# Second block's attention: value products issued ahead of the scores two units on

## The chip, the cores and the metric

The kernel is one program on one core of a Trainium2 chip. The metric is the device time of one execution in microseconds (us). The engines are named as in the profile: PE is TensorE (matrix products; PEld is its weight load), DVE is VectorE, ACT is ScalarE, POOL is GpSimd, and SP issues the transfers. Each engine runs its own list of instructions in the order in which the program gives them, and engines wait for each other on semaphores.

## What is computed

Two transformer blocks in a row, each with two layers, all in float32: 256 latent tokens and 256 context tokens, 1024 features. The first block (a gated recurrence, then attention over a compressed key) is not touched. The change is in the attention of the second block, which stands once in each of its two layers. Its reference, cut to what matters:

```python
def latent_attention(q, k, v, kc, vc, sink):          # 8 query heads, 2 key heads, head width 64
    s_lat = einsum(qb, kb) * scale                     # banded: |q - k| <= 128
    s_lat = where(valid, s_lat, NEG_INF)
    s_ctx = einsum(qb, kc) * scale
    p = softmax(concat([s_lat, s_ctx, sink]))          # the sink is one more column
    o = p_lat @ vb + p_ctx @ vc

for l in range(2):
    o = latent_attention(q, k, v, kc, vc, attn_sink[l])
    x = x + g1 * merge_branches(o, pool, fourier, gates, ...)
    if l == 0:
        oc = context_attention(qc, kc, vc, attn_sink[l])   # the context attends to itself
        xc = xc + cg1 * merge_branches(oc, ...)
    x = x + g2 * conv_ffn(...)
```

## The kernel before

The order on every engine is written out by hand; no scheduler moves anything. Activations lie with features on the 128 partitions. Weights come through a ring of buffers that SP fills ahead (`L128` in the rows).

The attention of layer `l` is cut into **units** (`att_units`, L863). A unit is a pair of heads `j` (0 to 3) and a block of 128 query rows `g` (2, 3: latent), or `g == 0`, which holds both blocks of the context. Layer 0 has 12 units, in the order 0, 2, 3 for each `j`, so units 0, 3, 6, 9 are context units; layer 1 has 8, all latent. Each unit goes through these steps:

- scores (PE, `att_scores_tensor`): L892 and L894 for a latent unit, L887 for a context unit, into bank 2+3 or 4+5 of `ps`, by the parity of the unit. They wait for `s_exp` of the unit two before, which had the same banks.
- top (DVE, `att_top_vector`): the row maximum L1672 straight from `ps`, then L1673 and L1674.
- exponentials (ACT, `exps`, L1327 and L1329), into `sc`.
- normalising (DVE, L1682, L1683, L1686), which raises `p_ready`.
- transposes (PE, L984): eight, the four of the first head into bank 6, those of the second into bank 1.
- copies out of these two banks into `PTb`: bank 6 always by ACT (L1342); bank 1 by ACT (L1345) for even units, by DVE (L1693) for odd ones. They raise `pt_kept` and `k_turned`.
- values (PE, `values`, L968): the products with the value rows, from `PTb` into bank 7 or 0. They wait for both copies of their own unit. After the last unit of a pair of heads ACT copies the result out (`heads_out`, L1333).

There is one `PTb`, and one bank for the transposes of each head. So the transposes of unit u+1 wait for the copies of u, and the copies of u+1 for the values of u.

DVE's order in `attend_vector` (L1676) matters here: for unit u it normalises u, then takes the top of u+2, and only then, if u is odd, makes the copy out of bank 1:

```python
                ins.then_inc(p_ready, 1)
                if u + 2 < len(units):
                    att_top_vector(dve, st, l, u + 2)
                if u % 2:
                    dve.wait_ge(pt_full, b["ptf"] + 2 * u + 2)
                    dve.wait_ge(pv_full, b["pv"] + u)
                    V.tensor_copy(PTb[:, 1, :], ps[:, 1, :]).then_inc(k_turned, 1)
```

ACT's order in `attend_scalar` is: exponentials of u+1, copy of bank 6 of u, for even u the copy of bank 1, then `heads_out` where a pair has ended. After its loop over the units PE runs `between()`, the first products of the Fourier branch (L994), ahead of the last unit's values, then the branches (L1007 to L1023) and the merge (L1040, L1052).

Of the kernel before, what the change touches and what calls it, by code (L numbers as in the profile page):

```python
# [42 lines left out]
def raised(n):  # L43


    return n + 1
# [89 lines left out]
def build(nc, w, const, out):  # L136
# [5 lines left out]
    with ctx:  # L142
# [715 lines left out]
        def base(l):  # L858
            return dict(unit=32 + 12 * l, ptf=32 + 24 * l, kt=12 * l, pv=8 + 12 * l, rot=9 + 3 * l, qj=1 + 3 * l, pvk=8 + 4 * l,
                        full=5 * l, act=5 * l, dve=3 + 5 * l, br=12 * l, brd=6 * l, bract=4 * l)  # L860


        def att_units(l):  # L863
            return [(j, g) for j in range(4) for g in ((0, 2, 3) if l == 0 else (2, 3))]
# [4 lines left out]
        def att_out(j):  # L869
            return 7 if j % 2 == 0 else 0  # L870

        def att_scores_tensor(pe, l, u):

            b = base(l)
            j, g = att_units(l)[u]
            bank = att_banks(u)
            if u >= 2:
                pe.wait_ge(s_exp, b["unit"] + u - 1)
            elif u == 1:
                pe.wait_ge(qj_ready, b["qj"] + 3)  # L880
            else:
                pe.wait_ge(qj_ready, b["qj"] + 2)
            head = lambda h2: slice(h2 * 64, h2 * 64 + 64)
            if g == 0:
                for gc in range(2):
                    for h2 in range(2):
                        mm = PE.matmul(ps[:, bank + h2, gc * CTX:gc * CTX + CTX], q_raw[head(h2), j, gc * 128:gc * 128 + 128],  # L887
                                       kb[head(h2), 0:CTX], start=True, stop=True)
            else:
                q0 = CTX * (1 - l) + (g - 2) * 128  # L890
                for h2 in range(2):
                    PE.matmul(ps[:, bank + h2, :], q_raw[head(h2), j, q0:q0 + 128], kb[head(h2), :], start=True, stop=False)  # L892
                for h2 in range(2):
                    mm = PE.matmul(ps[:, bank + h2, (5 - g) * 128:(5 - g) * 128 + 128], ident, amask[:, g - 2, :],  # L894
                                   start=False, stop=True)
            mm.then_inc(s_full, 1)
# [57 lines left out]
        def attend_tensor(pe, l, between):  # L954
            b = base(l)
            units = att_units(l)
            head = lambda h2: slice(h2 * 64, h2 * 64 + 64)

            def values(u):
                j, g = units[u]  # L960
                pe.wait_ge(pt_kept, raised(b["unit"] + u + 1))
                pe.wait_ge(k_turned, b["kt"] + u + 1)
                if j >= 2:
                    pe.wait_ge(pv_kept, raised(b["pvk"] + j - 1))
                nk, nq, q0 = (2, 256, 0) if g == 0 else (4, 128, g * 128)
                for kg in range(nk):
                    for h2 in range(2):
                        mm = PE.matmul(ps[head(h2), att_out(j), q0:q0 + nq], vb[:, kg, head(h2)], PTb[:, h2, kg * nq:kg * nq + nq],  # L968
                                       start=kg == 0, stop=kg == nk - 1)
                mm.then_inc(pv_full, 1)  # L970

            pe.wait_ge(in_dve_kept, b["dve"] + 5 - 2 * l)
            for u, (j, g) in enumerate(units):
                if u + 2 < len(units):
                    att_scores_tensor(pe, l, u + 2)
                if u:
                    values(u - 1)
                pe.wait_ge(p_ready, b["unit"] + u + 1)
                for h2 in range(2):
                    if u:  # L980
                        pe.wait_ge(*((pt_kept, raised(b["unit"] + u)) if h2 == 0 else (k_turned, b["kt"] + u)))
                    for n in range(4):
                        dst = n if g else n % 2 * 2 + n // 2
                        mm = PE.transpose(ps[:, (6, 1)[h2], dst * 128:dst * 128 + 128], sc[:, u % 2, h2, n * 128:n * 128 + 128], ident)  # L984
                    mm.then_inc(pt_full, 1)
            between()
            values(len(units) - 1)
# [117 lines left out]
        def _(pe):  # L1105
# [73 lines left out]
            for l in range(2):  # L1179
                n, c0 = T - CTX * l, CTX * l  # L1180
                norm_tensor(pe, f"mix{l}", lambda k: hT[:, k, :], ones, T)
                in_tensor(pe, l)
                attend_tensor(pe, l, lambda: spectra_tensor(pe, l))
                branches_tensor(pe, l)
                merge_tensor(pe, l)
                out_tensor(pe, l)
                norm_tensor(pe, f"ffn{l}", lambda k: hT[:, k, 0:n], ones, n)
                up_tensor(pe, l)
                pe.wait_ge(conv_ready, FT * (l + 1))
                outer_tensor(pe, f"down{l}", lambda k: hid[:, k, 0:n], n, FT, x_added, XB[f"down{l}"],  # L1190
                             lambda k: pe.wait_ge(hid_ready, raised(FT * l + k + 1)))
# [816 lines left out]
```

## Time and profile before

| | us |
|---|---|
| median of three runs | 2806.47 (2806.2 to 2807.56) |
| the profiled execution | 2807.16 |
| its span in the trace | 2805.4 |
| PE busy in it | 2631.2 (94%) |
| DVE busy | 898.9 (32%) |
| ACT busy | 591.8 (21%) |

The attention of layer 0 lies at about 1484 to 1532 us of the span, that of layer 1 at about 2362 to 2394 us. A line of the timeline gives the start in us, the duration in us, the engine, the line of the kernel, the operation, what it writes and reads, the shape, and how many instructions are merged in it; in brackets stands the idle time of the engine ahead of it and what ended it. The trace counts a float32 matrix product of the program as two records, a transpose as one.

### The profile page before, as it was taken

The page shows a single profiled execution, that of the slowest core. Times are in us where ns is not written, and L with a number is a line of the kernel's source. Part 1 is how long each engine was busy: PE and PEld are TensorE (multiplying, and loading weights), DVE is VectorE, ACT ScalarE, POOL GpSimd, SP SyncE. Part 2 cuts the span into 40 slices and gives each one's busy share as a digit, 9 for nine tenths or more (in the row PEclk, how much of TensorE's full clock was granted, in tenths as well). Part 3 has the DMA queues.
Part 4 walks back from the last instruction along what each step waited for, and adds up shares of the span by engine and source line. Part 5 has one row for each costly group of instructions (what it writes and reads, how often), then busy time and mean ns, then how long its engine had stood idle before and what let it go on. Part 6 is the DMA issues. An engine that isn't in the chain of part 4 may idle for free.

```text
span 2805.4 us, 27549 instructions
## 1 busy us (share of the span) xinstructions
PE 2631.2 (94%) x10670; PEld 1627.7 (58%) x10670; DVE 898.9 (32%) x1457; ACT 591.8 (21%) x1017; POOL 52.9 (2%) x42
## 2 busy tenths in 40 slices
PE   7999999999997878899799999999998989999988
PEld 3556666666665435666566444444443437888877
DVE  2236446446446221353115010132322014113321
ACT  3112222212211111242115000032221013103321
POOL 0000000000000100000000000000000000000000
PEclk9999999999998989999999999999999999999999
DMA  8443343333340313112420222222224222343561
GB/s 296 164 152 120 130 138 129 126 134 142 112 135 1 113 30 105 53 37 75 120 60 1 60 60 90 60 60 75 75 75 118 77 60 61 103 154 102 150 183 57
DMA packets 319687, 280.10 MB, mean 100 GB/s; under 512 B 27601, under 2 KB 298585, under 8 KB 319497
## 3 DMA queue, kind: packets, MB, share of 16 engines
q1 hardware_dynamic: 317866, 274.89, 31.9%
q0 software_dynamic: 1280, 4.20, 0.4%
q8 instruction: 45, 0.74, 0.1%
q10 hardware_dynamic: 479, 0.13, 0.0%
q14 instruction: 17, 0.14, 0.0%
HBM read 278.15 MB, written 1.05 MB: 100 GB/s over the span
## 4 chain that ended last, share of the span: by engine, by line
PE 93%; DVE 4%; ACT 2%; issue 1%; DMA 0%; SPq 0%; ACTq 0%; DVEq 0%
PE ps L1094 16%; PE ps L610 16%; PE ps L735 13%; PE ps L1040 9%; PE ps L619 4%; PE ps L657 4%; PE ps L1074 3%; PE ps L1052 3%; PE ps L398 2%; PE ps L345 2%; PE ps L770 2%; PE ps L942 1%; PE ps L920 1%; PE ps L699 1%; DVE rstd L350 1%; PE ps L847 1%
## 5 line engine op out<-in xcount | busy, mean ns | idle before, releaser
L1094 PE MATMUL ps<-hT,ring_mem 128*128 128x512 f32 (+1 forms) x1408 | 458.2, 489 | 9.8 <-ACT hT L411 9.8
L610 PE MATMUL ps<-hT,ring_mem 128*128 128x512 f32 x1024 | 454.4, 597 | 6.4 <-ACT hT L411 6.4
L735 PE MATMUL ps<-arena,ring_mem 128*128 128x256 f32 (+1 forms) x1160 | 375.1, 487 | 22.6 <-issue 14.8
L1094 PEld LDWEIGHTS ps<-hT,ring_mem 128*128 128x128 f32 x1408 | 269.4, 191 | 198.6 <-issue 178.1
L610 PEld LDWEIGHTS ps<-hT,ring_mem 128*128 128x128 f32 x1024 | 190.8, 191 | 238.8 <-issue 237.0
L735 PEld LDWEIGHTS ps<-arena,ring_mem 128*128 128x128 f32 x1160 | 223.5, 193 | 173.9 <-issue 148.1
L1040 PE MATMUL ps<-hT,ring_mem 128*128 128x512 f32 (+1 forms) x768 | 250.3, 486 | 0.0
L1040 PEld LDWEIGHTS ps<-hT,ring_mem 128*128 128x128 f32 x768 | 146.0, 190 | 101.3 <-issue 91.3
L1760 DVE SCALAR_TENSOR_TENSOR arena<-ps,vecs,arena 128x510 f32<-128x510 f32 (+1 forms) x176 | 100.2, 611 | 314.4 <-ACT arena L1385 308.1
L657 PEld LDWEIGHTS ps<-arena,K_c 128*128 128x128 f32 x896 | 115.6, 193 | 23.6 <-issue 22.9
L1722 DVE TENSOR_TENSOR arena<-ps,arena 128x512 f32<-128x512 f32 (+1 forms) x48 | 26.8, 558 | 291.3 <-PE ps L1052 291.3
L657 PE MATMUL ps<-arena,K_c 128*128 128x128 f32 x896 | 118.1, 286 | 0.0
L1732 DVE SCALAR_TENSOR_TENSOR xT<-ps,mod_b,xT 128x256 f32<-128x256 f32 (+1 forms) x48 | 21.8, 481 | 294.9 <-PE ps L735 225.6
L619 PE MATMUL ps<-ring_mem,hT 128*128 128x256 f32 x512 | 113.0, 379 | 0.0
L619 PEld LDWEIGHTS ps<-ring_mem,hT 128*128 128x128 f32 x512 | 96.2, 190 | 12.4
L332 ACT ACTIVATE hT<-xT 128x512 f32<-128x512 f32 (+1 forms) x56 | 26.4, 554 | 361.9 <-DVE xT L1732 333.4
L1231 ACT ACTIVATE K_c<-arena 128x1024 f32<-128x1024 f32 x56 | 64.0, 1144 | 183.0 <-DVE arena L1491 160.4
L350 DVE RECIPROCAL rstd<-root 128x512 f32<-128x512 f32 (+1 forms) x11 | 30.5, 2771 | 215.7 <-ACT root L337 215.7
L1491 DVE TENSOR_TENSOR arena<-arena 128x1024 f32<-128x1024 f32 x56 | 76.3, 1363 | 64.1 <-PE ps L657 64.0
L1052 PE MATMUL ps<-arena,ring_mem 128*128 128x512 f32 (+1 forms) x256 | 85.2, 486 | 0.0
L1074 PE MATMUL ps<-arena,ring_mem 128*128 128x512 f32 (+1 forms) x256 | 82.9, 486 | 0.0
L1385 ACT ACTIVATE arena<-ps,vecs 128x512 f32<-128x512 f32 (+1 forms) x88 | 46.3, 576 | 173.4 <-PE ps L1094 173.1
(227 smaller groups left out, 2553.3 us busy)
## 6 DMA issues: line engine op xcount, KB each, us to landing
ring_mem<-in_w_mod_dram SPq DMA_DIRECT2D x24, 2048.0 KB, 7.6
ring_mem<-in_w_up_dram SPq DMA_DIRECT2D x88, 512.0 KB, 4.8
ring_mem<-in_hg_w_in_dram SPq DMA_DIRECT2D x40, 1024.0 KB, 5.0
ring_mem<-in_w_in_dram SPq DMA_DIRECT2D x30, 1024.0 KB, 5.4
ring_mem<-in_w_down_dram SPq DMA_DIRECT2D x16, 1408.0 KB, 7.3
ring_mem<-in_ada_w_dram SPq DMA_DIRECT2D x8, 2048.0 KB, 7.7
ring_mem<-in_mla_w_in_dram SPq DMA_DIRECT2D x9, 1024.0 KB, 5.5
ring_mem<-in_ada_w_dram SPq DMA_DIRECT2D x8, 1024.0 KB, 10.4
```

The costliest lines, as they stand in the source:

```text
L350: st.link(V.reciprocal(rstd[:, 0:n], root[:, 0:n]))
L610: mm = PE.matmul(bank, wj[:, k, m * 128:m * 128 + 128], hT[:, k, :], start=k == 0, stop=k == 7)
L619: mm = PE.matmul(bank[:, g * 256:g * 256 + 256], hT[:, k, tok:tok + 128], wj[:, k, :], start=k == 0, stop=k == 7)
L657: mm = PE.matmul(dst, K_c[:, u * 128:u * 128 + 128], comb(Qw, 1 << (term - 1), u), start=True, stop=True)
L735: mm = PE.matmul(ps[:, j, 0:n], wj[:, k, :], src(k), start=k == 0, stop=k == kts - 1)
L1040: mm = PE.matmul(ps[:, j, 0:n], wj[:, k, m * 128:m * 128 + 128], hT[:, k, c0:T], start=k == 0, stop=k == 7)
L1052: mm = PE.matmul(ps[:, 3 + j, 0:n], wj[:, k, m * 128:m * 128 + 128], brT[:, k, c0:T], start=k == k0, stop=k == k1 - 1)
L1074: mm = PE.matmul(ps[:, 2 * j + m, 0:n], wj[:, k, m * 128:m * 128 + 128], yT[:, k, c0:T], start=k == 0, stop=k == 7)
L1094: mm = PE.matmul(ps[:, 2 * j + m, 0:n], wj[:, k, m * 128:m * 128 + 128], hT[:, k, c0:T], start=k == 0, stop=k == 7)
L1231: S.activation(view(K_c, (2 * h, PC // (2 * h)), (h, 2), (1, h)), comb(Kw, h), ACT.Copy).then_inc(kc_ready, 1)
L1491: V.tensor_tensor(comb(Qw, h), comb(Qw, h), view(Tw, (2 * h, n), (PC - h, 2), (0, h), at=h), ALU.mult).then_inc(merged, 1)
L1760: ins = V.scalar_tensor_tensor(dst, src, tap(k, f, part), dst, ALU.mult, ALU.add)
```

## The change

In the loop over the units of `attend_tensor`, the call `values(u - 1)` is put ahead of `att_scores_tensor(pe, l, u + 2)`; before it stood behind it. What each waits for, what each computes, and the order on the other engines stay.

```diff
             for u, (j, g) in enumerate(units):
+                if u:
+                    values(u - 1)
                 if u + 2 < len(units):
                     att_scores_tensor(pe, l, u + 2)
-                if u:
-                    values(u - 1)
                 pe.wait_ge(p_ready, b["unit"] + u + 1)
```

PE's list, before, at the start of layer 0's loop: the transposes of unit 0, scores of 3, values of 0, transposes of 1, scores of 4 (two rows), values of 1, transposes of 2. L984 are transposes, L968 values, L887 or L892 with L894 scores.

```order
269 L984 MATMUL ps<-ident,arena 128x128 x8
270 L887 MATMUL ps<-arena 128x256 x4
271 L968 MATMUL ps<-arena 64x256 x4
272 L984 MATMUL ps<-ident,arena 128x128 x8
273 L892 MATMUL ps<-arena 128x512 x2
274 L894 MATMUL ps<-arena,ident 128x128 x2
275 L968 MATMUL ps<-arena 64x128 x8
276 L984 MATMUL ps<-ident,arena 128x128 x8
```

The same place of the same engine in the changed kernel:

```order
269 L984 MATMUL ps<-ident,arena 128x128 x8
270 L968 MATMUL ps<-arena 64x256 x4
271 L887 MATMUL ps<-arena 128x256 x4
272 L984 MATMUL ps<-ident,arena 128x128 x8
273 L968 MATMUL ps<-arena 64x128 x8
274 L892 MATMUL ps<-arena 128x512 x2
275 L894 MATMUL ps<-arena,ident 128x128 x2
276 L984 MATMUL ps<-ident,arena 128x128 x8
```

The scores stood between a unit's transposes and its values; now they stand between its values and the next transposes.

PE's list at the end of layer 0's loop, before (values of 8, transposes of 9, values of 9, and so on to the transposes of 11):

```order
299 L892 MATMUL ps<-arena 128x512 x2
300 L894 MATMUL ps<-arena,ident 128x128 x2
301 L968 MATMUL ps<-arena 64x128 x8
302 L984 MATMUL ps<-ident,arena 128x128 x8
303 L968 MATMUL ps<-arena 64x256 x4
304 L984 MATMUL ps<-ident,arena 128x128 x8
```

and in the changed kernel:

```order
299 L968 MATMUL ps<-arena 64x128 x8
300 L892 MATMUL ps<-arena 128x512 x2
301 L894 MATMUL ps<-arena,ident 128x128 x2
302 L984 MATMUL ps<-ident,arena 128x128 x8
303 L968 MATMUL ps<-arena 64x256 x4
304 L984 MATMUL ps<-ident,arena 128x128 x8
```

Here only the scores of unit 11 moved, to just ahead of the transposes of unit 9; from row 302 on both lists are alike.

DVE's list, alike in both, around the copy of unit 1 (L1693): the normalising of 1, the top of 3, the copy, the normalising of 2.

```order
490 L1686 TENSOR_SCALAR arena<-arena 128x512 x2
491 L1672 TENSOR_REDUCE arena<-ps 128x4
492 L1673 SCALAR_TENSOR_TENSOR arena<-arena 128x4
493 L1674 TENSOR_TENSOR arena<-arena,sink 128x4
494 L1693 COPY arena<-ps 128x512
495 L1682 TENSOR_TENSOR arena<-arena 128x2
```

The lists of DVE, ACT, POOL and SP have the same rows in both kernels.

## Rows read from the trace of the kernel before

**Rows 1.** Stretches: us, busy time by engine (instructions), granted PE clock, DMA share, GB/s.

```profile
1490.00:1518.00 28.00, 28.00 (x238) 18.81 (x235) 24.47 (x67) 20.13 (x66) 0.00 (x0) 1.00 0.00 1
```

**Rows 2.** Timeline of PE, layer 0: first transposes, then two periods of the loop.

```profile
1485.53 1.04 PE L984 MATMUL ps<-ident,arena 128*128 128x128 f32 x8
...
1492.34 1.09 PE L984 MATMUL ps<-ident,arena 128*128 128x128 f32 x8
1493.36 1.13 PE L892 MATMUL ps<-arena 64*128 64x512 f32 x4
1494.42 0.71 PE L894 MATMUL ps<-arena,ident 128*128 128x128 f32 x4
1495.06 1.10 PE L968 MATMUL ps<-arena 128*64 128x128 f32 x16
1496.09 1.09 PE L984 MATMUL ps<-ident,arena 128*128 128x128 f32 x8
1497.11 1.14 PE L887 MATMUL ps<-arena 64*128 64x256 f32 x8
1498.18 1.08 PE L968 MATMUL ps<-arena 128*64 128x256 f32 x8
1499.19 1.09 PE L984 MATMUL ps<-ident,arena 128*128 128x128 f32 x8
```

**Rows 3.** Timeline of PE, end of layer 0's loop: units 9, 10, 11, then the branch.

```profile
1517.29 1.09 PE L984 MATMUL ps<-ident,arena 128*128 128x128 f32 x8
1519.21 1.08 PE L968 MATMUL ps<-arena 128*64 128x256 f32 x8 [0.83 <-ACT arena L1342]
1520.35 1.09 PE L984 MATMUL ps<-ident,arena 128*128 128x128 f32 x8
1522.23 1.09 PE L968 MATMUL ps<-arena 128*64 128x128 f32 x16 [0.79 <-ACT arena L1342]
1523.26 1.09 PE L984 MATMUL ps<-ident,arena 128*128 128x128 f32 x8
1524.19 7.03 PE L994 MATMUL ps<-arena 128*128 128x512 f32 x16
```

**Rows 4.** Timeline, scores of unit 2 straight ahead of transposes, and their top.

```profile
1484.98 0.71 PE L894 MATMUL ps<-arena,ident 128*128 128x128 f32 x4
...
1485.73 1.22 DVE L1672 TENSOR_REDUCE arena<-ps 128x2 f32<-128x1024 f32 x1 [0.40 <-PE ps L894]
```

**Rows 5.** Timeline of DVE: a copy behind a top, and one that waited for PE.

```profile
1488.45 1.22 DVE L1672 TENSOR_REDUCE arena<-ps 128x4 f32<-128x1024 f32 x1
...
1489.98 0.69 DVE L1693 COPY arena<-ps 128x512 f32<-128x512 f32 x1
...
1518.42 0.69 DVE L1693 COPY arena<-ps 128x512 f32<-128x512 f32 x1 [0.43 <-PE ps L984]
1519.03 0.15 DVE L1682 TENSOR_TENSOR arena<-arena 128x2 f32<-128x2 f32 x1
```

**Rows 6.** Timeline, layer 0's loop end: the normalising of 11, ACT's second copy of 10.

```profile
1520.92 0.88 DVE L1686 TENSOR_SCALAR arena<-arena 128x512 f32<-128x512 f32 x2
...
1521.54 0.59 ACT L1345 ACTIVATE arena<-ps 128x512 f32<-128x512 f32 x1
```

**Rows 7.** Timeline of PE, layer 1: transposes of unit 0 and of unit 6.

```profile
2363.66 1.09 PE L984 MATMUL ps<-ident,arena 128*128 128x128 f32 x8 [1.20 <-DVE arena L1686]
...
2385.47 1.09 PE L984 MATMUL ps<-ident,arena 128*128 128x128 f32 x8
```

**Rows 8.** Stretches elsewhere, columns as in rows 1, and a timeline row of PE.

```profile
920.00:925.00 5.00, 3.43 (x31) 3.24 (x30) 2.64 (x10) 0.00 (x0) 0.00 (x0) 1.00 0.00 0
...
922.76 4.73 PE L699 MATMUL ps<-arena 128*128 128x128 f32 x40 [1.57 <-DVE arena L1510]
```

**Rows 9.** A stretch at the lower clock, columns as in rows 1.

```profile
1405.00:1410.00 5.00, 3.42 (x4) 1.51 (x5) 0.31 (x2) 4.65 (x10) 0.00 (x0) 0.50 0.00 0
```

**Rows 10.** Waits of PE after layer 0's attention: total us, times, longest; first of four.

```profile
PE ps L735 <- issue: 7.5, 1, 7.5
```

## The prediction

> **What bounds the kernel now.** I read first how busy each engine is, then the timeline of PE through both attentions, then that of DVE and ACT beside it. In the loop of layer 0 PE is busy 28.00 of 28.00 us at a granted clock of 1.00, while DVE works 24.47 and ACT 20.13 us [rows 1]. So PE sets the pace there, and any time in which it waits is added to the kernel. The timeline shows how the order of before manages this. From the transposes of a latent unit to the next thing on PE it takes 1.02 us (1492.34 to 1493.36), the scores take 1.06 and 0.64, the values 1.03, and a period is 3.75 us (1492.34 to 1496.09); a period with a context unit's scores is 1.02 + 1.07 + 1.01 = 3.10 (1496.09 to 1499.19) [rows 2]. Between transposes and values stand the scores, 1.07 or 1.70 us of work, and in that time ACT and DVE make the copies that the values need.
>
> How much those copies take is seen where this cover is missing, at the end of the loop, since units 10 and 11 issue no further scores. Unit 9's values start 1.92 us behind the start of its transposes (1517.29 to 1519.21), unit 10's 1.88 us (1520.35 to 1522.23), where 1.02 would do [rows 3]. The change makes this the rule in every unit.
>
> **Part 1: even units (copies on ACT alone).** Their values will start 1.88 us after their transposes, as in unit 10: ACT makes its second copy from 1.19 us after the transposes (1521.54 against 1520.35), and the values come 0.69 us behind that start (1522.23) [rows 3, 6]. I assume ACT is free by then; its exponentials of u+1 were released by scores that now come a full period of at least 3.97 us earlier, and they and the copies need about 3 to 4 us in all, 20.13 us in seven to eight periods [rows 1]. If that cover failed, the next copies would be late by the rest of an exponential, some tenths each.
>
> **Part 2: odd units (copy of bank 1 on DVE).** DVE's list has the top of u+2 ahead of the copy of u. Before, the scores of u+2 were done before the values of u-1, a microsecond ahead of the transposes, and the top was over when the copy's turn came: in unit 9 the copy waited for PE, started 1.13 us after the transposes (1518.42) and released the values 0.79 us later [rows 3, 5]. Now those scores end just where the transposes start, so the top starts only then. Where scores already stood straight ahead of transposes, it started 0.75 us after L894, and the transposes 0.55 us after it (1485.53), hence 0.20 us after the start of the transposes [rows 2, 4]. From the start of a top to that of a copy queued behind it is 1.53 us (1488.45 to 1489.98) [rows 5]. So the copy starts 1.73 us after the transposes, and the values 1.73 + 0.79 = 2.52. I use this for scores of a context unit too. DVE is free for the top: the normalising of u has to be over for the transposes of u to start at all.
>
> **Part 3: what is saved.** Latent scores followed by transposes take 1.06 + 0.55 = 1.61 us, not 1.70 [rows 2, 4]. From values to transposes of the next unit it is then 1.02 + 1.61 = 2.63 us over latent scores, and 1.02 + 1.07 = 2.09 over context scores.
>
> **The sum for layer 0**, from the start of one transposes to the next:
> - units 0 and 6 (even, scores of a context unit follow): 1.88 + 2.09 = 3.97
> - units 2, 4, 8: 1.88 + 2.63 = 4.51
> - units 1, 5, 7: 2.52 + 2.63 = 5.15
> - unit 3 (odd, context scores): 2.52 + 2.09 = 4.61
> - unit 9: no scores behind it, but its copy is now late as in part 2. Here DVE is next in line: the copy starts at 1.73, the normalising of 10 starts 0.61 us later (1518.42 to 1519.03) and the transposes 1.32 us after that (1520.35) [rows 3, 5]: 3.66 us, against 3.06 before.
> - unit 10: as before.
>
> That is 2 x 3.97 + 3 x 4.51 + 3 x 5.15 + 4.61 + 3.66 = 45.19 us. Before, transposes 0 to 10 took 1485.53 to 1520.35 = 34.82 us [rows 2, 3]. Layer 0 loses 10.37 us.
>
> **Layer 1**, eight latent units: 3 x 4.51 (0, 2, 4) + 2 x 5.15 (1, 3) + 3.66 (unit 5, the last with scores just ahead of its transposes) = 27.49 us, against 2363.66 to 2385.47 = 21.81 [rows 7]. It loses 5.68 us.
>
> Together 16.05 us. The transposes of a unit do not become late for another reason: the normalising of u+1 follows the copy of u on DVE, which in odd units puts the transposes at 3.66 us at the earliest, and the shortest odd period is 4.61. After the loop PE's list is the same; everything behind it moves as a block. The chance of a gain in these parts I exclude but for part 3, since PE had no idle time there that an earlier value product could fill [rows 1].
>
> **A point on reading idle time.** The timeline marks 0.83 and 0.79 us of idle ahead of the uncovered values, but the start-to-start times say 1.92 - 1.02 = 0.90 and 1.88 - 1.02 = 0.86 [rows 3]. I use the starts. The Trainium skill, Perfetto Trace Analysis, section "Tensor Engine Instruction (MATMUL, LD_WEIGHTS)", states that a matrix product's start is reported while its end is computed from its size, so idle ahead of a product is a difference with a modelled end. By the idle marks the sum would be some 1.0 us smaller (0.07 in each of 14 waits); this trace bears the page out, the two readings differ by 0.07 us, and a start is what the next product depends on.
>
> **The rivals.**
> 1. *The small loss.* DVE's copy is not late, so every odd unit has 1.92 as in unit 9 before and not 2.52. Layer 0 would then lose 0.60 less in units 1, 3, 5, 7 and in 9, layer 1 in 1, 3 and 5: 8 x 0.60 = 4.8 us less, 11.3 us in all, time 2817.7. For it speaks only that no top is seen right behind transposes in an odd unit of before; against it that DVE's list fixes top before copy and a top takes 1.22 us [rows 5].
> 2. *The clock.* PE would now pause 0.86 to 1.50 us in every 4 to 5 us. If the granted clock fell, every product would take up to twice as long: at 0.50 four products of 512 columns are busy 3.42 us, 0.86 each, and at 1.00 sixteen take 7.03, 0.44 each [rows 3, 9]. PE's work in the two loops is some 35 + 22 us, so a third of it at the lower level adds 19 us (2841), all of it 57 (2880). Against it: with PE busy 3.43 of 5 us and a pause of 1.57 us ahead of one group, the clock stayed at 1.00 [rows 8], and that pause is longer than the longest that I expect.
> 3. *No loss: ready scores run ahead of blocked values.* If PE let products whose operands are there pass those that wait, the scores would fill the pause as before, whatever the list says, and the time would be within 1 us of before: 2806. It decides from the first even unit on. Against it: the transposes of unit 11 had their operand normalised at 1520.92 + 0.88 = 1521.80, and bank 6 free before, yet PE stood until 1522.23, did the values of 10, and only then began them, at 1523.26 [rows 3, 6].
> 4. *The loss is given back later.* It would need a place where PE afterwards waits for something that does not move with it, a transfer above all. Between layer 0's attention and layer 1's the list of PE's waits has four entries, the longest 7.5 us, none on a transfer [rows 10]; they are norms that start only when PE's own results are there. To come within 5.6 us of before, over 10 us would have to come back: 2812 or less.
>
> **How the numbers follow.** The profiled execution took 2807.16 us for a span of 2805.4; with 16.05 it would take 2823.2. It lies 0.7 above the median 2806.47, and I put the change on the median: 2822.5 us.
>
> Chances: the forecast 0.86, the small loss 0.06, the clock 0.04, no loss 0.03, given back 0.01. Forecast, small loss and clock are all slower by over 5.6 us, which is 0.2% of the time and about what a measurement of this kernel can tell from no change: slower 0.96, same 0.03, faster 0.01 (from the last, should more than the loss come back).
>
> The range: at the low end the small loss, 2817.7, less half a microsecond of spread between runs. At the high end the forecast without part 3 (11 scores x 0.09 = 1.0 us, as values in place of transposes might start as late as before) and with another 0.1 us of waiting in each of 16 units (1.6), 2825.1, and the spread of the runs of before, 1.4 us, with a microsecond for ACT's cover: 2817.2 to 2827.5. It leaves out the clock and both cases of no loss.
>
> **What would show it.** In the changed trace PE's values (L968) should show an idle time of about 0.8 us ahead of them in every even unit, put down to ACT's L1345 or L1342, and about 1.4 us in odd ones, put down to DVE's L1693; periods between transposes of 4.5 and 5.15 us in turn for latent scores; DVE's L1672 starting 0.2 us after the transposes and L1693 1.7 us after them; no idle ahead of L892 or L887; the clock at 1.00. Transposes 0 to 10 of layer 0 should span 45 us, 0 to 6 of layer 1 27.5. The prediction is wrong in its second part if L1693 starts 1.1 us after the transposes, in its first if the even units' values start more than 2 us after them, and in its frame if the stretches after the attention are shorter than before.

## The result, and the profile after

| | before | changed |
|---|---|---|
| median | 2806.95 us (4 runs, 2806.2 to 2807.56) | 2823.93 us (4 runs, 2823.45 to 2826.34) |
| profiled execution | 2807.16 us | 2826.34 us |
| span | 2805.4 us | 2824.6 us |
| transposes of unit 0 to those of unit 10, layer 0 | 34.82 us | 45.06 us |
| transposes of unit 0 to those of unit 6, layer 1 | 21.81 us | 27.58 us |

The change costs 17.0 us by the medians, a ratio of 1.0062 (95% interval 1.0045 to 1.008), so it is small but clear of the noise. The two loops lose 10.24 and 5.77 us in the trace, 16.01 together.

The same stretch as in [rows 1], of the changed kernel. Columns: us, busy time of PE, PEld, DVE, ACT and POOL, each with its instructions, then granted clock, DMA share, GB/s.

```profile
1490.00:1518.00 28.00, 21.09 (x178) 14.36 (x176) 18.40 (x50) 15.90 (x50) 0.00 (x0) 1.00 0.01 2
```

PE is idle for 6.9 of 28 us where it had been idle for none. DVE and ACT are less busy too, since the same work of each unit is now spread over a longer period. The clock stayed at 1.00, so the loss is waiting alone. Next, PE's timeline in the loop of layer 0, which answers to [rows 2]; the columns are those given there, with the idle time ahead of a group in brackets.

```profile
1491.21 1.09 PE L984 MATMUL ps<-ident,arena 128*128 128x128 f32 x8
1493.70 1.09 PE L968 MATMUL ps<-arena 128*64 128x128 f32 x16 [1.40 <-DVE arena L1693]
1494.72 1.13 PE L892 MATMUL ps<-arena 64*128 64x512 f32 x4
1495.78 0.71 PE L894 MATMUL ps<-arena,ident 128*128 128x128 f32 x4
1496.33 1.04 PE L984 MATMUL ps<-ident,arena 128*128 128x128 f32 x8
1498.20 1.09 PE L968 MATMUL ps<-arena 128*64 128x128 f32 x16 [0.83 <-ACT arena L1345]
1499.22 1.13 PE L892 MATMUL ps<-arena 64*128 64x512 f32 x4
1500.28 0.71 PE L894 MATMUL ps<-arena,ident 128*128 128x128 f32 x4
1500.83 1.04 PE L984 MATMUL ps<-ident,arena 128*128 128x128 f32 x8
1503.40 1.08 PE L968 MATMUL ps<-arena 128*64 128x256 f32 x8 [1.53 <-DVE arena L1693]
```

Every value product (L968) now has idle time ahead of it. In turn it is ended by DVE's copy (units 1 and 3: 1.40 and 1.53 us) and by ACT's (unit 2: 0.83 us). Nothing stands idle ahead of the scores or the transposes. The waits of PE over the whole kernel, columns: total us, times, longest.

```profile
PE ps L968 <- DVE arena L1693: 7.5, 5, 1.5
...
PE ps L968 <- issue: 4.3, 3, 1.5
PE ps L968 <- ACT arena L1345: 4.1, 5, 0.8
PE ps L968 <- ACT arena L1342: 3.9, 5, 0.8
```

That is 19.8 us of waits in 18 places, where the kernel before had the four at the loops' ends, of which [rows 3] show two. The three put down to "issue" are waits of odd units like the five above them; their length says so. Why the odd units wait longer stands on DVE, at unit 3 of the changed kernel; these rows answer to [rows 4, 5].

```profile
1501.03 1.22 DVE L1672 TENSOR_REDUCE arena<-ps 128x2 f32<-128x1024 f32 x1 [1.42 <-PE ps L894]
...
1501.96 0.59 ACT L1333 ACTIVATE arena<-ps 128x512 f32<-128x512 f32 x1
...
1502.56 0.69 DVE L1693 COPY arena<-ps 128x512 f32<-128x512 f32 x1
```

The transposes of unit 3 start at 1500.83. DVE starts the top of unit 5 at once behind its scores, 0.20 us later, having stood idle for 1.42 us; the copy follows at 1.73 us and the values at 2.57 (1503.40). The bank that the copy reads was full by about 1.1 us, for the copy that waited for PE in [rows 5] started 1.13 us behind its transposes. In an even unit, 2, ACT's second copy starts 1.13 us behind the transposes (1496.33), and the values come 0.74 us later (1498.20):

```profile
1497.46 0.59 ACT L1345 ACTIVATE arena<-ps 128x512 f32<-128x512 f32 x1
```

The profiled execution of the changed kernel lies 19.2 us of span above that of before, 3.2 more than the loops. It is the slowest of its four. The first transposes of layer 0 start 1.74 us later than before (1487.27), ahead of any changed instruction, and 1.4 us more lie between the two loops. The repeat below says whose these are.

### The profile page after: what moved, and what is told of

It is laid out like the page before. It is cut to its first block, busy times and chain, and to the rows that moved or that the text cites. A ratio compares the mean times of both kernels' runs of the same rounds, so it can differ in the third digit from the quotient of the medians.

```text
span 2824.6 us, 27549 instructions
## 1 busy us (share of the span) xinstructions
PE 2632.7 (93%) x10670; PEld 1626.8 (58%) x10670; DVE 899.1 (32%) x1457; ACT 593.1 (21%) x1017; POOL 53.0 (2%) x42
## 4 chain that ended last, share of the span: by engine, by line
PE 91%; DVE 4%; ACT 2%; issue 1%; DMA 1%; SPq 0%; ACTq 0%; DVEq 0%
PE ps L1094 16%; PE ps L610 16%; PE ps L735 13%; PE ps L1040 9%; PE ps L619 4%; PE ps L657 4%; PE ps L1074 3%; PE ps L1052 3%; PE ps L398 2%; PE ps L345 2%; PE ps L770 2%; PE ps L942 1%; PE ps L920 1%; PE ps L699 1%; PE ps L847 1%
## 5 line engine op out<-in xcount | busy, mean ns | idle before, releaser
L735 PE MATMUL ps<-arena,ring_mem 128*128 128x256 f32 (+1 forms) x1160 | 377.8, 489 | 23.4 <-issue 15.6
L735 PEld LDWEIGHTS ps<-arena,ring_mem 128*128 128x128 f32 x1160 | 224.3, 194 | 176.6 <-issue 150.7
```

The source lines that it names most:

```text
L735: mm = PE.matmul(ps[:, j, 0:n], wj[:, k, :], src(k), start=k == 0, stop=k == kts - 1)
```

## Experiments

Each kernel differs from the kernel before or from the changed one by one edit. The loops' figures are starts of transposes, as in the table above. Kernels that were measured together share their runs of the kernel before; ratios are given with their 95% intervals.

### Was the odd units' extra wait DVE's order? ACT makes all copies

In the changed kernel:

```diff
-                if u % 2 == 0:
-                    act.wait_ge(pt_full, b["ptf"] + 2 * u + 2)
-                    S.activation(PTb[:, 1, :], ps[:, 1, :], ACT.Copy).then_inc(k_turned, 1)
+                act.wait_ge(pt_full, b["ptf"] + 2 * u + 2)
+                S.activation(PTb[:, 1, :], ps[:, 1, :], ACT.Copy).then_inc(k_turned, 1)
...
-                if u % 2:
-                    dve.wait_ge(pt_full, b["ptf"] + 2 * u + 2)
-                    dve.wait_ge(pv_full, b["pv"] + u)
-                    V.tensor_copy(PTb[:, 1, :], ps[:, 1, :]).then_inc(k_turned, 1)
```

> The changed kernel, with bank 1 copied to PTb by ACT in odd units too, as in even ones; DVE's copy is gone. Theory (an odd unit's values wait 2.52 us behind their transposes because DVE takes the top of u+2 ahead of its copy): every unit is now like an even one, values 1.9 us behind the transposes, periods 4.5 us for latent scores and 4.0 for context scores in odd units too; transposes 0 to 10 of layer 0 span 42.0 us (after: 45.1, before: 34.8), 0 to 6 of layer 1 25.6 (27.6, 21.8); the loss against before falls from 16.0 to about 11.0 us, time about 2818. Rival (the longer wait of odd units is latency of the transposes' bank 1 or of DVE's read, not DVE's order, and ACT's second copy would be as late): 45 and 27.5 us stay, time 2823.

Measured: 41.92 and 25.57 us for the loops, a median of 2819.06 us against 2808.11 (ratio 1.0038, 1.0024 to 1.0053), so +10.95 us. PE's timeline of that kernel at the values of unit 3:

```profile
1500.13 1.04 PE L984 MATMUL ps<-ident,arena 128*128 128x128 f32 x8
1502.00 1.08 PE L968 MATMUL ps<-arena 128*64 128x256 f32 x8 [0.83 <-ACT arena L1344]
```

The wait is 1.87 us from transposes to values where it was 2.57, and the rest of the loss remains. Five of the 16 us (3.1 and 2.0 in the two loops) go when DVE's copy goes, as the theory had it. One half of the rival, a bank that is full late, falls: ACT's second copy of the same bank is not late. The other half, a slow read by DVE, is not tried here, since DVE no longer reads. The kernel with DVE's copy ahead of the top (below) settles it: there DVE still copies, and the odd units' values start 1.86 to 1.97 us behind the transposes.

### The same edit in the kernel before

> The kernel before, with the same edit. Control: before, scores cover the copies, so it is worth nothing in the loop; at the loops' ends, where DVE's copy of the last odd unit with a successor stood ahead of the normalising, about 0.15 us each. Transposes 0 to 10 of layer 0 span 34.7 us, time within 0.5 us of before. Rival (ACT's load matters by itself, 20 of 28 us busy before): the loop grows, by up to 0.5 us in each odd unit, 4 us in all.

Measured: 34.65 and 21.64 us, median 2806.73 against 2808.11 (ratio 0.9996, 0.9986 to 1.0005), no difference that the runs can tell. The loops are 0.17 us shorter each, all of it in the last odd unit with a successor (2.89 us where it was 3.06), as expected. With the scores as cover it does not matter which engine copies, nor that ACT does more. What an engine's order costs depended on the cover above it.

### The opposite: DVE makes all copies of bank 1

In the changed kernel, ACT's copy of bank 1 is dropped and DVE's condition `if u % 2` too.

> The changed kernel, with bank 1 copied by DVE in every unit, behind the top of u+2; the opposite of the first run. Theory: every unit now waits as an odd one, 2.52 us from transposes to values. Periods 5.15 (latent scores) and 4.6 (context scores) in even units too: transposes 0 to 10 of layer 0 span 48.4 us (+13.6 against before), 0 to 6 of layer 1 29.4 (+7.6), together +21.2, time about 2828. The rival of the clock: pauses of 1.4 to 1.5 us now stand in every period, PE busy under three quarters of the time; in the run with the copy first the granted clock fell to 0.51 behind pauses of 0.83 and 1.57 us. If density decides, it falls here in the loops too, and the time is above 2832.

Measured: 48.82 us (+14.0) and 29.28 us (+7.5), median 2828.57 against 2807.45 (ratio 1.0076, 1.006 to 1.0093), so +21.1 us.

```profile
1504.56 1.09 PE L984 MATMUL ps<-ident,arena 128*128 128x128 f32 x8
1507.04 1.09 PE L968 MATMUL ps<-arena 128*64 128x128 f32 x16 [1.40 <-DVE arena L1689]
```

An even unit (4) now waits like an odd one, 2.48 us. Layer 0's loop took 0.4 us more than expected. Most of it is in unit 6, whose period is 4.97 us: its copy starts 2.09 us behind the transposes and not 1.73, after 0.28 us in which DVE waited for nothing that the profile shows. The cause of that stays open. The three kernels with the same order on PE give +11.0, +17.0 (the change; the prediction's sum had 16.05) and +21.1 us with none, half and all of the second copies behind DVE's top. And with PE busy about 7 of 10 us through both loops (33.84 of 49 us and 25.67 of 36) the granted clock stayed at 1.00; one stretch of it:

```profile
1490.00:1500.00 10.00, 7.07 (x64) 4.79 (x62) 6.52 (x18) 4.76 (x16) 0.00 (x0) 1.00 0.00 1
```

### One half of the change at a time

In the kernel before, the values go first in odd turns only (which are the values of even units), or in even turns only:

```diff
+                first = u % 2 == 1          # the other kernel: == 0
+                if u and first:
+                    values(u - 1)
                 if u + 2 < len(units):
                     att_scores_tensor(pe, l, u + 2)
-                if u:
+                if u and not first:
                     values(u - 1)
```

> Values ahead of the scores only for even units' values (odd turns of the loop); odd units' values stay behind the scores. Theory: even units have periods of 4.5 (latent scores) and 4.0 us (context scores); odd ones have scores as cover for 2.7 us, more than the 2.52 of the late copy, so 3.75, but units 3 and 5 of layer 0 are held by DVE to about 3.66 and 3.94, and the last one with a successor is 3.66. Layer 0's transposes 0 to 10: 40.2 us (+5.4), layer 1's 0 to 6: 24.7 (+2.9), together +8.3 us, time 2815. Rival (no effect of DVE's order; 0.76 to 0.87 for each exposed unit and nothing else): +6.3 us.

Measured: 40.30 and 24.67 us (+5.5, +2.9), median 2815.92 against 2808.11 (ratio 1.0028, 1.0018 to 1.0039), +7.8 us. The periods of units 3 and 5 are 3.67 and 3.94, where 3.66 and 3.94 were expected. In unit 3 the cover is there but too short: only a context unit's scores stand ahead of the values, the late copy lets them start 2.58 us behind the transposes, and PE waits 0.47 us for it.

> Values ahead of the scores only for odd units' values (even turns). Theory: the scores of u+2 for an odd u then still come before the values of u-1, so DVE's top is over when its copy is due; odd units' values start 1.92 us behind the transposes, not 2.52, periods 4.55 (unit 3: 4.0), even ones stay 3.75 and 3.1. Layer 0 +3.3 us (38.1), layer 1 +1.6 (23.4), together +4.9, time 2812. With the even units' +8.3 that makes 13.2, not 16.0: the rest needs both at once. Rival (an odd unit costs 1.4 us whenever its values are ahead): +9 us, and the two halves add to 16 or more.

Measured: 38.63 and 23.39 us (+3.8, +1.6), median 2812.24 against 2808.11 (ratio 1.0017, 1.0007 to 1.0026), +4.1 us. Layer 0 lost 0.5 us more than expected, in units 1 and 7, whose periods are 4.86 and 4.81 and not 4.55. The rows at unit 1 of this kernel (the line numbers are three higher on DVE: L1689 normalises, L1675 is the maximum, L1696 the copy; L987 are the transposes):

```profile
1487.42 0.88 DVE L1689 TENSOR_SCALAR arena<-arena 128x512 f32<-128x512 f32 x2
...
1488.22 1.22 DVE L1675 TENSOR_REDUCE arena<-ps 128x4 f32<-128x1024 f32 x1
1488.36 1.09 PE L987 MATMUL ps<-ident,arena 128*128 128x128 f32 x8
...
1489.75 0.69 DVE L1696 COPY arena<-ps 128x512 f32<-128x512 f32 x1
```

The scores were done, but DVE was still normalising unit 1 until just before the transposes, so the top began only 0.14 us ahead of them and the copy came at 1.39 us. For this run I had expected the top to be over when the copy was due. It is not where a short period of 3.06 us precedes. The kernel before shows the same, unnoticed, because scores cover it there: the copy of unit 1 starts at 1489.98 [rows 5], also 1.39 us behind its transposes, which start here:

```profile
1488.59 1.09 PE L984 MATMUL ps<-ident,arena 128*128 128x128 f32 x8
```

The halves add to 13.7 us in the loops, the whole is 16.0. The rest belongs to both together: an odd unit's copy is at its latest only if the scores of u+2 are late, and that costs in full only if the odd unit's values have no cover.

### DVE's copy ahead of the top

In the changed kernel, the copy stands ahead of `att_top_vector(dve, st, l, u + 2)`. It was measured twice, each time beside the kernel before.

> The changed kernel, with DVE's copy of an odd unit ahead of the top of u+2. Theory: the odd units' values start 1.92 us behind the transposes, but the top, and behind it the normalising of u+1, are now later by the copy's wait and 0.6 us: 1.13 + 0.61 + 1.53 + 1.32 = 4.59 us to the next transposes (4.87 where u+1 is a context unit), so DVE takes the place of the wait. Layer 0's transposes 0 to 10: 44.7 us (after: 45.1), layer 1's 27.3 (27.6); loss 15.4 to 15.7, time about 2822.5. Rival (the order of copy and top is the whole of the odd units' extra wait): the loss falls to 11.3, time 2818.

> The kernel with DVE's copy ahead of the top, once more. Does the fall of the granted clock at the end of layer 1's loop (transposes of unit 6 to the start of the Fourier products, some 2.8 us lost) come again? If it belongs to the pattern of pauses, it shows again here or at the end of layer 0's loop and the time is 2825 to 2826; if it was one execution's, the clock is 1.00 throughout the loops and the profiled time about 2822.7.

Measured: the loops are 44.59 and 27.21 us in both executions (expected 44.7 and 27.3). Moving the copy forward does shorten its own wait: in unit 1 the values start 1.96 us behind the transposes. But the top and the next normalising are later, and they hold the next transposes. What it gives the loops, 0.8 us, is no remedy. The medians are 2825.74 against 2808.25 (ratio 1.0065, 1.005 to 1.0081) and 2822.01 against 2807.45 (ratio 1.0055, 1.0038 to 1.0071). The first is 2.2 us above the changed kernel that was measured with it (below), and its trace shows why its profiled execution was slow; the other three have no trace. Stretches at the end of layer 1's loop, columns as above:

```profile
2396.00:2401.00 5.00, 3.22 (x32) 2.23 (x28) 2.70 (x7) 1.25 (x4) 0.00 (x0) 1.00 0.00 0
2402.00:2408.00 6.00, 5.27 (x32) 4.53 (x31) 1.32 (x5) 2.07 (x4) 0.00 (x0) 0.50 0.00 0
```

and PE's timeline there:

```profile
2398.96 1.09 PE L968 MATMUL ps<-arena 128*64 128x128 f32 x16 [0.83 <-ACT arena L1342]
...
2401.62 1.60 PE L984 MATMUL ps<-ident,arena 128*128 128x128 f32 x8 [1.57 <-DVE arena L1686]
...
2405.86 1.97 PE L984 MATMUL ps<-ident,arena 128*128 128x128 f32 x8
```

The clock stood at its lower level, 1.2 GHz, for over 6 us, and eight transposes took 1.97 us in place of 1.09. From the transposes of unit 6 to those of unit 7 it took 4.24 us and not 2.90, and to the last values of the layer 10.16 us where the repeat takes 7.36, so the fall cost 2.8 us. In the repeat the same waits stand in the same places and the clock is 1.00 throughout, that period 2.90. The same pauses, 0.83 and then 1.58 us, stand at the end of layer 0's loop in both executions too, at 1.00. So the clock fell behind this pattern at one of four places. That the pauses brought it down is not shown, and what decides it between two executions of one program these traces don't show.

### The changed kernel once more

> The changed kernel once more, beside the others on the same chip. The two loops lose 10.2 and 5.8 us in the trace; if what the first profiled execution had beyond these 16.0 us (19.2 us of span) belongs to that execution and not to the change, the stretches ahead of layer 0's loop and between the two loops are here within 0.5 us of before, and the time is 2822 to 2824. If it belongs to the change, 1.7 us ahead of the first loop and 1.4 between the loops come again.

Measured: median 2823.55 against 2808.25 (ratio 1.0056, 1.0041 to 1.0071), +15.3 us; loops 45.06 and 27.58, to the hundredth those of the first execution. Layer 0's first transposes start at 1485.64 (before: 1485.53), and between the loops, from transposes 10 to transposes 0, lie 843.23 us (before 843.31; first execution of the changed kernel 844.70). The 1.7 and 1.4 us were the execution's own. The kernel before with ACT's copies, alike up to there, also starts its first transposes 1.5 us late (1487.02).

Behind layer 1's loop, from the values of unit 6 to the products of the next norm (L345), it is 150.34 us in the kernel before and in both executions of the changed one. In the last long run of products (L735) the repeat takes 77.92 us where the kernel before takes 79.17, which is why its span is 14.8 us above that of before and not 16.0. This is no gain of the change: its first execution has 79.16, and the kernel before with ACT's copies 77.63.

### Cover for the places that had none before

If ready work between transposes and values is what counts, the kernel before can still gain at the two ends of its loops. The first Fourier products (L994 before, L999 here) are ready there; in place of all behind the last transposes, a part goes behind each of the last three.

```diff
                 if u + 2 < len(units):
                     att_scores_tensor(pe, l, u + 2)
+                elif u + 2 == len(units):
+                    pe.wait_ge(s_exp, b["unit"] + u + 1)
+                    between(0)
+                else:
+                    between(1)
                 if u:
                     values(u - 1)
...
-            between()
+            between(2)
...
+            steps = [(ct, s, st) for ct in range(2) for s in range(l, 2) for st in range(2)]
+            cuts = (0, 2, 4, 8) if l == 0 else (0, 2, 3, 4)
+            for i in range(cuts[part], cuts[part + 1]):
```

> The kernel before, with the first Fourier products (L994) spread as cover over the last three transposes of each layer, where no scores are left: those of bank 2 behind the transposes of the third last unit (with a wait on the exponentials of the second last, which used that bank), the next behind the second last, the rest behind the last. Nothing is left out. Theory (any ready PE work between transposes and values hides the copies): the waits of 0.83 and 0.79 us ahead of L968 go in both layers, and with 0.1 of DVE's in each of the first; 1.9 us a layer, 3.8 in all, time about 2803. Rival (what is bound there is the chain through DVE's normalising, not the cover): the waits move ahead of L984, and the time stays within 1 us of before.

Measured: median 2804.25 against 2808.25 us (ratio 0.9986, 0.9977 to 0.9995), -4.0 us, where 3.8 were expected: faster than both kernels. The traces give 1.87 us in layer 0 and 1.85 in layer 1, from the first transposes to the branch behind the last values (46.54 us to 44.67, and 30.09 to 28.24). PE's timeline at the place of [rows 3] (L989 are the transposes):

```profile
1517.67 1.09 PE L989 MATMUL ps<-ident,arena 128*128 128x128 f32 x8
1518.60 1.88 PE L999 MATMUL ps<-arena 128*128 128x512 f32 x4
1520.42 1.08 PE L968 MATMUL ps<-arena 128*64 128x256 f32 x8
1521.43 1.09 PE L989 MATMUL ps<-ident,arena 128*128 128x128 f32 x8
1522.36 1.88 PE L999 MATMUL ps<-arena 128*128 128x512 f32 x4
1524.17 1.09 PE L968 MATMUL ps<-arena 128*64 128x128 f32 x16
```

No idle time is left ahead of the values, nor ahead of the transposes, so at these periods of 3.76 us the chain through DVE's normalising was no bound.

## Why the prediction was right, point by point

The forecast was 2822.5 us, 16.05 us above the median then known; measured are 2823.93, 17.0 above the median of the joint runs, and 15.3 in the repeat. The range held it. The mechanism is the one that was forecast: values that wait for copies without cover, and odd units that wait longer by DVE's order.

- **Part 1, even units.** Values 1.88 us behind the transposes were expected; they are 1.87 in unit 2 (1496.33 to 1498.20). ACT was free for its copies, as assumed. The figure given for that was not what its row says: 20.13 us in seven to eight periods are 2.5 to 2.9 us each, not "3 to 4". The true figure leaves more room, and no term rests on it. The run with all copies on ACT shows this term alone: 11.0 us.
- **Part 2, odd units.** Expected: top at 0.20, copy at 1.73, values at 2.52 us. Measured in unit 3: 0.20, 1.73, 2.57; from the copy to the values it took 0.84 us and not 0.79. That the copy was late by DVE's order is shown by the runs with all copies on ACT and all on DVE, and that DVE's copy is not slow by itself by the run with the copy first. With context scores, where I had used the latent figure, unit 1 has 2.49.
- **Part 3, the saving.** Scores L894 to transposes take 0.55 us (1495.78 to 1496.33), as expected.
- **The sum.** 10.37 and 5.68 us were expected, 10.24 and 5.77 measured. Unit 9, held by DVE, took 3.67 us against 3.66 expected. That the two loops come within 0.04 us of the forecast is in part luck, for the terms are off by up to 0.08 us and cancel. ACT's second copy was put at 1.19 us and the values 0.69 behind it, and they are at 1.13 and 0.74. Odd units over latent scores took 5.07 to 5.21 us (5.15 expected), even ones 4.45 to 4.55 (4.51), units 0 and 6 took 3.94 and 3.90 (3.97). By the idle marks the forecast would have been some 15.0 us for the loops; the 16.01 bear out the reading by starts.
- **One sentence of part 2 is too wide:** that before the change the top was over when the copy's turn came. It is true of unit 9 and not of unit 1, whose copy starts 1.39 us behind the transposes in the kernel before and not 1.13; under the scores this cost nothing. The forecast does not use it, but my expectation for the kernel with only odd values exposed did, and it missed by 0.3 us in units 1 and 7. The sentence that DVE is free for the top holds, since it speaks of the time from the start of the transposes, and in unit 3 of the changed kernel DVE stands idle for 1.42 us ahead of the top.
- **Rival 1, the small loss**, is refuted by the waits put down to L1693 and is what the kernel with ACT's copies is: I priced it at 11.3 us, and it measured 10.95.
- **Rival 2, the clock.** It did not happen in the changed kernel, nor with PE busy 7.07 of 10 us. I argued from one pause of 1.57 us in the trace of before at a clock of 1.00; that evidence was weaker than it looked, since a pause of 1.57 us was followed by the lower clock in one execution of another kernel. That the clock stays up under such pauses was not shown by it.
- **Rival 3, ready scores passing blocked values,** is refuted: the scores of unit 4 waited with the values of unit 1, 1.40 us.
- **Rival 4, given back later,** is refuted by the repeat, whose stretch between the loops is that of before within 0.1 us, and by the 150.34 us behind layer 1's loop. The prediction took all four waits of [rows 10] for norms; the row shown, the longest, is put down to "issue", so it does not say what ended that wait.

## What to carry to other kernels

On an engine that runs its list in order and sets the pace, the place between a product and the consumer of its copied result belongs to independent work at least as long as the copy (here 0.9 us of wait, covered by 1.07 or 1.70 us of scores); work moved behind the consumer covers nothing. Price such a gap from a place in the same trace where the cover happens to be missing, such as the last turns of a loop, and then follow the moved work to the other engines: its result also arrived later, and a copy queued behind the instruction that reads that result cost the last third of the loss.

## What was not expected of the hardware

In one execution the granted clock of PE went from 1.00 to 0.50 for over 6 us behind pauses of 0.83 and 1.57 us, which cost 2.8 us. Another execution of the same program, with the same pauses, stayed at 1.00, and so did the kernel in which DVE makes all copies, with pauses of 1.13 to 1.85 us in every period of both loops. The other surprise is how exact start-to-start times were: both loops of the changed kernel took 45.06 and 27.58 us in two executions whose spans differ by 4.4 us.
